# A decoder layer on one core: the last two column chunks of the last down projection by seven products

## The chip, the core and the metric

One of the eight cores of a Trainium2 chip runs the whole kernel. The metric is the device time of one execution in microseconds (us). Engines: TensorE (PE; its loads of stationary data are PEld) multiplies into eight PSUM banks; VectorE (DVE) and ScalarE (ACT) work element by element; GpSimd (POOL) here issues only transfers that add to what their destination holds; SyncE (SP) issues plain transfers. Each engine runs its own list of instructions in order and waits on semaphores.

## The reference, cut to what matters

The layer is attention and then a ConvFFN, on 256 rows of 2048 columns in float32. What the change touches is the last line:

```
h = rms_norm(x, g_ffn)
u = h @ w_up                        # 2048 x 11264
conv = sum(wc[t] * shift(u, t)) + b_conv
gate, val = split(conv)
x = x + (silu(gate) * val) @ w_down # 5632 x 2048
```

## The kernel before

**Float32 from three products.** Every operand is kept as a high part (rounded to the multiplier's format) and a low part (the difference). A product of a 128x128 block of activations with a 128x512 block of weights is three matmuls: high with high, high with low of the weights, low of the activations with high. ScalarE rounds each weight tile (`high`, w_hi), VectorE makes the difference (`low`, w_lo), both six units ahead of TensorE (`RING = 6`). A weight tile is 256 rows by 512 columns, 512 KB.

**The down projection.** The 5632 hidden columns are 11 blocks of 512 (`BLOCKS`), counted 0 to 10. Of each block, the product with w_down has four column chunks of 512, each of two units ("D", block, u): u = 0..7, chunk u // 2, half u % 2 of the block's 512 hidden columns. A unit is 2 row tiles x 2 blocks of 128 hidden columns x 3 = 12 matmuls, and its weight tile is `w_down[block, u]`. The sums of a chunk are added by VectorE (`add_down`) to `xr`, the residual stream in SBUF (part of `work`), and for the last block SyncE then stores them.

**Seven products.** The up projection already uses a scheme with seven products in place of eight, on 2x2 blocks: activations (rows 0-127 or 128-255, by two column groups) and weights (two sides by two groups). Its steps are called P1 to P7. Some need sums of activations, made by VectorE, then rounded by ScalarE and split by VectorE (`part_high`/`part_low`, `make_more` in block 1); some need sums of weight tiles, made in the buffers `x_at` and `y_at` (raw_x, raw_y, and parts of odd and work), by VectorE or by GpSimd's adding transfers. P1, P6 and P5 add up in one bank, and ScalarE copies out what it holds after P1 and after P6 before the next one writes there. In block 1 half a plain unit stands between P6 and P5.

**What sets the order.** `ffn_units` writes out by hand one list of units for the whole feed-forward part, and every engine walks that list. At unit n, ScalarE and VectorE first do what empties banks, then round and split the weights of unit n + 6, then what else stands at that unit (convolution taps, hidden activations). At the end stand block 9's down units 2 to 7 (from its unit 3 on nothing between them), then block 10's units 0 to 7. Block 10's hidden activations are made meanwhile: VectorE's `hidden` and `hidden_low` and ScalarE's `hidden_high` stand at block 9's units 3 and 4.

**Loads.** `LOADS` are the units with plain tiles; six slots take them in turn (softmax, consts_sb, raw 0 to 3), and SyncE issues a slot's next load when VectorE has split the tile in it.

Of the kernel before, what the change touches and what calls it, by code (L numbers as in the profile page):

```python
# [6 lines left out]
P = 128  # L7
SEQ = 256
RT = SEQ // P
# [192 lines left out]

def ffn_units():
# [46 lines left out]
    units += [("D", BLOCKS - 1, u) for u in range(UPR)]  # L250
# [6 lines left out]
LOADS = [unit for unit in FFN if unit[0] != "S"]  # L257
# [14 lines left out]
def slot_of(k):  # L272
    return FIRST_SLOTS[k % len(FIRST_SLOTS)]

# [43 lines left out]
def decoder_layer(nc, x, x_t, smalls, consts, w_in, w_fox, w_dil, w_out, w_up, w_down, decay_dram, out):  # L318
# [15 lines left out]
    with ctx:  # L334
# [125 lines left out]
        def last_half(name, half):  # L460

            if name in LAST_OWN:
                return own_more[:, LAST_OWN.index(name), :, half * P:half * P + P]
            return actB[:, 12:14, half * SEQ + P:half * SEQ + 2 * P]

# [126 lines left out]
        def _(sp):  # L592
# [64 lines left out]
            def load_unit(unit):  # L657
# [4 lines left out]
                elif unit[0] == "D":  # L662
                    src = w_down[unit[1], unit[2], :, :]
                else:
# [102 lines left out]
            for k in range(RAW_SLOTS):  # L767
                sp.wait_ge(lo_done, FF_UNIT - RAW_SLOTS + k)
                load_unit(LOADS[2 + k])
            for n, unit in enumerate(FFN, FF_UNIT):  # L770
                if unit[0] != "S":
# [13 lines left out]
                elif name == "P2" and i + 1 < BLOCKS:  # L785
# [21 lines left out]
            for c in range(4):  # L807
                for r in range(RT):
                    sp.wait_ge(d_added, 8 * (BLOCKS - 1) + 2 * c + r + 1)
                    sp.dma_start(out_rows[:, r, c * NB:(c + 1) * NB], xr[:, r, c * NB:(c + 1) * NB])\  # L810
                        .then_inc(out_done, 16)
# [4 lines left out]
        def _(pe):  # L816
# [460 lines left out]
            def down_pair(i, c):  # L1277

                at = 4 * (i - BLOCKS + 2) + c
                pairs = {2: (0, 1), 3: (2, 3), 4: (5, 6), 5: (0, 1), 6: (2, 3), 7: (4, 7)}.get(at, (5, 6))  # L1280
                return bank[pairs[0]], bank[pairs[1]]

            def down_unit(n, i, u):
# [3 lines left out]
                if u % 2 == 0:  # L1287
# [5 lines left out]
                    elif i == BLOCKS - 1 and c < 3:  # L1293
                        pe.wait_ge(d_added, 8 * i - 4 + 2 * c)
                    elif i == BLOCKS - 1:
                        pe.wait_ge(conv_done, 2 * BLOCKS)
# [4 lines left out]
                last = i == BLOCKS - 1 and u == UPR - 1  # L1301
# [3 lines left out]

            for n, unit in enumerate(FFN, FF_UNIT):
                if unit[0] == "D":
# [35 lines left out]
        def _(act):  # L1343
            def high(n):
# [24 lines left out]
                elif FFN[n - FF_UNIT][0] != "S":  # L1369
                    k = LOAD_AT[FFN[n - FF_UNIT]]  # L1370
                    src = raw_at[slot_of(k)]
                    act.wait_ge(w_loaded[slot_of(k)], 16 * load_count(k))
                else:
# [489 lines left out]

            for n, unit in enumerate(FFN, FF_UNIT):
                running_sum(n, unit)
                down_out(n, unit)
                if unit == ("U", 1, 1, 0):
                    seed_down(0, 0)
# [13 lines left out]
                elif unit == ("U", 0, 1, 0):  # L1882
                    act.wait_ge(warm, 2)
                    nc.scalar.activation(st[:, 91:92], st[:, 90:91], ACT.Silu)
                if unit[0] == "D":
# [58 lines left out]
        def _(dve):  # L1944
            def low(n):
# [9 lines left out]
                elif FFN[n - FF_UNIT][0] != "S":  # L1955
                    src = raw_at[slot_of(LOAD_AT[FFN[n - FF_UNIT]])]
                else:
# [5 lines left out]
                if (pair and name == "P2"  # L1963
                        or n >= FF_UNIT and FFN[n - FF_UNIT][2] == "P2" and not fourth_by_transfer(i, q)):
                    dve.wait_ge(lo_done, n)
                    nc.vector.tensor_tensor(y_at[q], y_at[q], x_at[q], ALU.add).then_inc(y_added[q], 1)
                elif (n >= FF_UNIT and FFN[n - FF_UNIT][2] == "P7"
                      or pair and name == "P7"):
# [484 lines left out]
            def down_banks(i, c):  # L2453

                at = 4 * (i - BLOCKS + 2) + c
                pairs = {2: (0, 1), 3: (2, 3), 4: (5, 6), 5: (0, 1), 6: (2, 3), 7: (4, 7)}.get(at, (5, 6))
                return bank[pairs[0]], bank[pairs[1]]

            def add_down(n, i, c):

                row0 = i == BLOCKS - 1 and c == 3
# [49 lines left out]

            for n, unit in enumerate(FFN, FF_UNIT):
                empty_banks(n, unit)
# [4 lines left out]
                low(n + RING)  # L2518
                if unit[0] == "D":
# [166 lines left out]


# [53 lines left out]
```

## Time and profile before

| | us |
|---|---|
| median of three runs (lowest, highest) | 1333.23 (1333.12, 1333.65) |
| the profiled execution's own time | 1333.53 |
| its span, first to last instruction | 1331.6 |
| TensorE busy | 1326.6 (100%), 6043 matmuls recorded |
| VectorE busy | 1139.4 (86%) |
| ScalarE busy | 953.0 (72%) |
| GpSimd busy | 161.0 (12%) |

A busy TensorE means that a matmul is somewhere in its pipeline; the spacing of starts tells how fast it runs. The chain of waits says which work ended last at each moment, followed back from the end. In a timeline a row's first number is the start from the span's beginning, the second how long the instruction took; instructions of one engine overlap a little at their ends, so the distance between starts is what one costs in a row of them. A bracket at a row's end is the engine's idle time before it and what ended it.

### The profile page before, as it was taken

The page shows a single profiled execution, that of the slowest core. Times are in us where ns is not written, and L with a number is a line of the kernel's source. Part 1 is how long each engine was busy: PE and PEld are TensorE (multiplying, and loading weights), DVE is VectorE, ACT ScalarE, POOL GpSimd, SP SyncE. Part 2 cuts the span into 40 slices and gives each one's busy share as a digit, 9 for nine tenths or more (in the row PEclk, how much of TensorE's full clock was granted, in tenths as well). Part 3 has the DMA queues.
Part 4 walks back from the last instruction along what each step waited for, and adds up shares of the span by engine and source line. Part 5 has one row for each costly group of instructions (what it writes and reads, how often), then busy time and mean ns, then how long its engine had stood idle before and what let it go on. Part 6 is the DMA issues. An engine that isn't in the chain of part 4 may idle for free.

```text
span 1331.6 us, 16497 instructions
## 1 busy us (share of the span) xinstructions
PE 1326.6 (100%) x6043; PEld 1100.1 (83%) x6043; DVE 1139.4 (86%) x1355; ACT 953.0 (72%) x1201; POOL 161.0 (12%) x179
## 2 busy tenths in 40 slices
PE   9999999999999999999999999999999999999998
PEld 7888888888888888888888888888888888888887
DVE  6868787888877876888688898999999999999996
ACT  6666666666665654667777878888888888888872
POOL 0121212021011000101010101111111102020200
PEclk9999999999999999999999999999999999999999
DMA  9877685758888665597879798999989899999952
GB/s 358 281 177 259 143 262 118 244 153 229 229 219 225 219 214 197 128 316 204 268 179 324 165 298 177 309 226 278 249 246 270 231 288 216 303 206 311 205 197 95
DMA packets 119007, 306.78 MB, mean 230 GB/s; under 512 B 11912, under 2 KB 13200, under 8 KB 118672
## 3 DMA queue, kind: packets, MB, share of 16 engines
q1 hardware_dynamic: 91760, 233.53, 50.6%
q0 software_dynamic: 22816, 68.17, 29.0%
q10 hardware_dynamic: 4352, 4.05, 1.0%
q8 instruction: 48, 0.79, 0.2%
q14 instruction: 31, 0.25, 0.1%
HBM read 303.60 MB, written 2.11 MB: 230 GB/s over the span
## 4 chain that ended last, share of the span: by engine, by line
PE 98%; DMA 0%; DVE 0%; ACT 0%; issue 0%; POOL 0%; ACTq 0%; POOLq 0%
PE acc L826 12%; PE acc L830 12%; PE acc L828 12%; PE acc L866 9%; PE acc L870 9%; PE acc L868 9%; PE acc L1053 4%; PE acc L1057 4%; PE acc L1055 4%; PE acc L1032 3%; PE acc L1028 3%; PE acc L1030 3%; PE acc L1220 1%; PE acc L851 1%; PE acc L847 1%; PE acc L849 1%
## 5 line engine op out<-in xcount | busy, mean ns | idle before, releaser
L1961 DVE TENSOR_TENSOR w_lo<-raw,w_hi 128x1024 fp32r<-128x1024 f32 x225 | 273.2, 1222 | 66.8 <-ACT w_hi L1396 66.0
L1396 ACT ACTIVATE w_hi<-raw 128x1024 fp32r<-128x1024 f32 x225 | 235.2, 1054 | 87.5 <-PE acc L830 49.4
L826 PE MATMUL acc<-w_hi,actA 128*128 128x512 f32 x596 | 234.7, 394 | 0.0
L830 PE MATMUL acc<-w_hi,actA 128*128 128x512 f32 x596 | 232.4, 390 | 0.0
L828 PE MATMUL acc<-w_lo,actA 128*128 128x512 f32 x596 | 232.0, 389 | 0.0
L1396 ACT ACTIVATE w_hi<-raw_y 128x1024 fp32r<-128x1024 f32 x152 | 158.1, 1058 | 76.4 <-PE acc L830 22.2
L1961 DVE TENSOR_TENSOR w_lo<-raw_y,w_hi 128x1024 fp32r<-128x1024 f32 x152 | 183.0, 1221 | 21.2 <-ACT w_hi L1396 19.6
L1961 DVE TENSOR_TENSOR w_lo<-raw_x,w_hi 128x1024 fp32r<-128x1024 f32 x114 | 137.6, 1223 | 44.7 <-ACT w_hi L1396 44.5
L1396 ACT ACTIVATE w_hi<-raw_x 128x1024 fp32r<-128x1024 f32 x114 | 117.5, 1051 | 42.9 <-DMA raw_x<-w_in 21.2
L830 PEld LDWEIGHTS acc<-w_hi,actA 128*128 128x128 f32 x596 | 111.9, 188 | 23.7
L828 PEld LDWEIGHTS acc<-w_lo,actA 128*128 128x128 f32 x596 | 112.0, 188 | 22.5
L826 PEld LDWEIGHTS acc<-w_hi,actA 128*128 128x128 f32 x596 | 111.9, 188 | 22.5 <-issue 0.2
L866 PE MATMUL acc<-w_hi,actB 128*128 128x512 f32 x296 | 116.1, 392 | 0.0
L870 PE MATMUL acc<-w_hi,actB 128*128 128x512 f32 x296 | 115.3, 389 | 0.0
L868 PE MATMUL acc<-w_lo,actB 128*128 128x512 f32 x296 | 115.2, 389 | 0.0
L1053 PE MATMUL acc<-w_hi,actA 128*128 128x512 f32 x224 | 88.3, 394 | 0.0
L1057 PE MATMUL acc<-w_hi,actA 128*128 128x512 f32 x224 | 87.3, 390 | 0.0
L1055 PE MATMUL acc<-w_lo,actA 128*128 128x512 f32 x224 | 87.2, 389 | 0.0
L1396 ACT ACTIVATE w_hi<-odd 128x1024 fp32r<-128x1024 f32 x63 | 66.3, 1053 | 19.0 <-PE acc L870 9.8
L1961 DVE TENSOR_TENSOR w_lo<-odd,w_hi 128x1024 fp32r<-128x1024 f32 x63 | 76.9, 1221 | 1.8 <-ACT w_hi L1396 1.8
L2437 DVE SCALAR_TENSOR_TENSOR work<-acc,smalls_sb,work 128x255 f32<-128x255 f32 (+1 forms) x176 | 72.6, 478 | 3.4 <-ACT work L1779 3.3
L2668 POOL DMA_DIRECT2D raw_y<-w_up x34 | 29.5, 867 | 377.0 <-DVE w_lo L1961 376.8
(344 smaller groups left out, 2739.2 us busy)
## 6 DMA issues: line engine op xcount, KB each, us to landing
raw<-w_in SPq DMA_DIRECT2D x101, 512.0 KB, 4.8
raw<-w_down SPq DMA_DIRECT2D x59, 512.0 KB, 5.7
raw_x<-w_up SPq DMA_DIRECT2D x44, 512.0 KB, 4.9
raw_y<-w_up POOLq DMA_DIRECT2D x34, 512.0 KB, 7.3
raw_x<-w_in SPq DMA_DIRECT2D x28, 512.0 KB, 3.9
odd<-w_up SPq DMA_DIRECT2D x27, 512.0 KB, 5.2
work<-w_up SPq DMA_DIRECT2D x24, 512.0 KB, 5.5
work<-w_up POOLq DMA_DIRECT2D x24, 512.0 KB, 8.0
```

Source lines behind the costliest of these rows:

```text
L826: nc.tensor.matmul(o, lhsT=a_h, rhs=w_hi[:, s, k, :], start=first and k == 0, stop=False, skip_group_check=onto_seed)
L828: nc.tensor.matmul(o, lhsT=a_h, rhs=w_lo[:, s, k, :], start=False, stop=False, skip_group_check=onto_seed)
L830: mm = nc.tensor.matmul(o, lhsT=a_l, rhs=w_hi[:, s, k, :], start=False, stop=last and k == KU - 1, skip_group_check=onto_seed)
L866: nc.tensor.matmul(o, lhsT=a_h, rhs=w_hi[:, s, k, :], start=first and k == 0, stop=False, skip_group_check=True)
L868: nc.tensor.matmul(o, lhsT=a_h, rhs=w_lo[:, s, k, :], start=False, stop=False, skip_group_check=True)
L870: mm = nc.tensor.matmul(o, lhsT=a_l, rhs=w_hi[:, s, k, :], start=False, stop=last and k == KU - 1, skip_group_check=True)
L1053: nc.tensor.matmul(o, lhsT=a_h, rhs=w_hi[:, s, k, :], start=side == 0 and j == 0 and k == 0, stop=False, skip_group_check=True)
L1055: nc.tensor.matmul(o, lhsT=a_h, rhs=w_lo[:, s, k, :], start=False, stop=False, skip_group_check=True)
L1057: mm = nc.tensor.matmul(o, lhsT=a_l, rhs=w_hi[:, s, k, :], start=False, stop=kt == KT - 1, skip_group_check=True)
L1396: nc.scalar.activation(w_hi[:, n % RING, :, :], src.rearrange("p (k n) -> p k n", k=KU), ACT.Copy).then_inc(hi_done, 1)
L1961: nc.vector.tensor_tensor(w_lo[:, n % RING, :, :], src.rearrange("p (k n) -> p k n", k=KU), w_hi[:, n % RING, :, :].bitcast(f32), ALU.subt ...
L2437: t = nc.vector.scalar_tensor_tensor(out=conv[:, j, lag:SEQ], in0=bank[(4, 7)[j // 2]][:, (j % 2) * SEQ:(j % 2 + 1) * SEQ - lag], scalar=s ...
```

## The change

Block 10's units 4 to 7 (chunks 2 and 3, four plain units) go. In their place stand seven products ("T", 10, name), in the order P1, P7, P6, P5, P2, P4, P3, between units 0, 1 (chunk 0) and units 2, 3 (chunk 1), which are now last. A product is one 128-row block by 256 hidden columns: 6 matmuls.

```
     units += [("D", BLOCKS - 2, u) for u in range(LATE - 1, UPR)]
-    units += [("D", BLOCKS - 1, u) for u in range(UPR)]
+    units += [("D", BLOCKS - 1, u) for u in range(2)]
+    units += [("T", BLOCKS - 1, name) for name in TAIL_STEPS]
+    units += [("D", BLOCKS - 1, u) for u in range(2, LATE)]
+TAIL_STEPS = ("P1", "P7", "P6", "P5", "P2", "P4", "P3")
+TAIL_BANKS = {"P1": 4, "P6": 4, "P5": 4, "P7": 7, "P4": 7, "P2": 2, "P3": 5}
+TAIL_TILE = {"P1": 4, "P2": 5, "P3": 7}
+TAIL_SUMS = {"P4": (0, (7, 6, 4, 5)), "P6": (1, (7, 6, 4)), "P7": (2, (7, 6)), "P5": (3, (4, 6))}
+TAIL_STORES = ((0, 0), (1, 0), (1, 3), (0, 2), (1, 2), (0, 3), (0, 1), (1, 1))
```

P1, P2 and P3 use plain tiles (4, 5, 7) out of the six slots. The other four use sums of two to four tiles, signs being left to the activations and to the adds at the end. A sum's first tile is loaded by SyncE into `x_at[q]` when that buffer's last use is over, the others are added to it by GpSimd, first one for all four sums, then the second and third:

```
+                elif name == "P2":
+                    if fourth_by_transfer(i, q):
+                        sp.wait_ge(lo_done, n)
+                    else:
+                        sp.wait_ge(y_added[q], added_before(i, q) + 2)
+                    load_tail_base(q)
...
+            for more in range(3):
+                for q, tiles in TAIL_SUMS.values():
+                    if more + 1 >= len(tiles):
+                        continue
...
+                    nc.gpsimd.dma_start(x_at[q], w_down[BLOCKS - 1, tiles[more + 1], :, :], accum_op=ALU.add)\
+                        .then_inc(x_summed[q], 16)
```

VectorE makes four sums of activations (`make_tail`), ScalarE rounds five parts (`tail_high`, into own_parts and wf), VectorE splits them (`tail_low`):

```
+                if unit == ("D", BLOCKS - 2, UPR - 2):
+                    make_tail()
+                elif unit == ("D", BLOCKS - 2, UPR - 1):
+                    for part in ("P1", "P7", "P6"):
+                        tail_low(part)
+                elif unit == ("D", BLOCKS - 1, 0):
+                    for part in ("P5", "P3"):
+                        tail_low(part)
```

TensorE waits at the products, and ScalarE copies banks between them:

```
+            def tail_product(n, name):
+                if name == "P1":
+                    pe.wait_ge(conv_done, 2 * BLOCKS)
+                elif name == "P6" or name == "P2":
+                    pe.wait_ge(p1_copied, BLOCKS + 1)
+                elif name == "P5":
+                    pe.wait_ge(g_v, PAIRS + 2)
+                elif name == "P4":
+                    pe.wait_ge(g_v7, PAIRS + 2)
+                elif name == "P3":
+                    pe.wait_ge(d_seeded, seeds_before(BLOCKS - 2, 0) + 1)
+                if name in TAIL_PARTS:
+                    pe.wait_ge(h_part_lo, 8 + TAIL_PARTS.index(name) + 1)
+                pe.wait_ge(lo_done, n)
...
+            def tail_copy(n, name):
+                act.wait_ge(used, n + 1)
+                if name == "P1":
+                    act.wait_ge(d_added, 8 * (BLOCKS - 1))
+                    nc.scalar.activation(bank[2], bank[4], ACT.Copy, scale=-1.0).then_inc(p1_copied, 1)
+                elif name == "P7":
+                    nc.scalar.activation(tmp[:, 1, :], bank[7], ACT.Copy).then_inc(g_v7, 1)
+                elif name == "P5":
+                    act.wait_ge(d_seeded, seeds_before(BLOCKS - 2, 0) + 1)
+                    nc.scalar.activation(xr[:, 0, 3 * NB:], bank[4], ACT.Copy).then_inc(g_u0, 1)
+                else:
+                    nc.scalar.activation(tmp[:, 0, :], bank[4], ACT.Copy, scale=-1.0).then_inc(g_v, 1)
```

Bank 5, which P3 fills, is first loaded by ScalarE with the residual; six one-bank sums on VectorE (`tail_sums`) replace the four two-bank adds of chunks 2 and 3.

VectorE's list before, from the adds of block 9's chunk 2 on (acc is PSUM, work holds the residual; w_lo rows are weight differences, of block 10's units 3 to 7):

```order
L2470 TENSOR_TENSOR work<-acc,work 128x512 [waits unit_used]
L2470 TENSOR_TENSOR work<-acc,work 128x512
L1961 TENSOR_TENSOR w_lo<-raw,w_hi 128x1024 [waits hi_done] x2
L2470 TENSOR_TENSOR work<-acc,work 128x512 [waits unit_used]
L2470 TENSOR_TENSOR work<-acc,work 128x512
L1961 TENSOR_TENSOR w_lo<-raw,w_hi 128x1024 [waits hi_done]
L1961 TENSOR_TENSOR w_lo<-softmax,w_hi 128x1024 [waits hi_done]
L2470 TENSOR_TENSOR work<-acc,work 128x512 [waits unit_used]
L2470 TENSOR_TENSOR work<-acc,work 128x512
L1961 TENSOR_TENSOR w_lo<-consts_sb,w_hi 128x1024 [waits hi_done]
```

and now (L2636 to L2641 are the four sums, L2649 the low part of P1's activations; the w_lo rows are those of P7, P6 and P5):

```order
L2590 TENSOR_TENSOR work<-acc,work 128x512 [waits unit_used]
L2590 TENSOR_TENSOR work<-acc,work 128x512
L2082 TENSOR_TENSOR w_lo<-odd,w_hi 128x1024 [waits hi_done]
L2082 TENSOR_TENSOR w_lo<-raw_x,w_hi 128x1024 [waits hi_done]
L2636 TENSOR_TENSOR work<-work 128x256 [waits a_ready]
L2638 TENSOR_TENSOR work<-work 128x256 [waits h_made]
L2639 TENSOR_TENSOR work<-work 128x256
L2641 TENSOR_TENSOR work<-work 128x256 [waits h_made]
L2590 TENSOR_TENSOR work<-acc,work 128x512 [waits unit_used]
L2590 TENSOR_TENSOR work<-acc,work 128x512
L2082 TENSOR_TENSOR w_lo<-work,w_hi 128x1024 [waits hi_done]
L2649 SCALAR_TENSOR_TENSOR own_parts<-work,own_parts 128x2x128 [waits h_part_hi]
```

The weight differences keep their places; between them and the adds stand the four sums, and the low part for P1 comes behind P5's weights.

ScalarE's list before, from the rounding of block 10's hidden activations (L1803) on; the w_hi rows are the weights of units 3 to 7:

```order
L1803 ACTIVATE actA<-work 128x4x256 [waits unit_used,a_ready]
L1396 ACTIVATE w_hi<-raw 128x1024 [waits unit_used,w_loaded1]
L1396 ACTIVATE w_hi<-raw 128x1024 [waits unit_used,w_loaded2]
L1396 ACTIVATE w_hi<-raw 128x1024 [waits unit_used,w_loaded3]
L1396 ACTIVATE w_hi<-softmax 128x1024 [waits unit_used,w_loaded8]
L1396 ACTIVATE w_hi<-consts_sb 128x1024 [waits unit_used,w_loaded9]
```

and now, from P6's weights (raw_x) on (L1956 are the five parts, L1964, L1966 and L1971 the copies of P1, P7 and P6; w_hi rows: P6, P5, P2, P4, P3, unit 2):

```order
L1482 ACTIVATE w_hi<-raw_x 128x1024 [waits unit_used,x_summed1]
L1956 ACTIVATE own_parts<-work 128x2x128 [waits a_ready]
L1956 ACTIVATE wf<-work 128x2x128 [waits h_made]
L1956 ACTIVATE own_parts<-work 128x2x128 [waits h_made] x3
L1482 ACTIVATE w_hi<-work 128x1024 [waits unit_used,x_summed3]
L1482 ACTIVATE w_hi<-raw 128x1024 [waits unit_used,w_loaded1]
L1482 ACTIVATE w_hi<-raw_x 128x1024 [waits unit_used,x_summed0]
L1964 ACTIVATE acc<-acc 128x512 [waits d_added,unit_used]
L1482 ACTIVATE w_hi<-raw 128x1024 [waits unit_used,w_loaded2]
L1966 ACTIVATE tmp<-acc 128x512 [waits unit_used]
L1482 ACTIVATE w_hi<-raw 128x1024 [waits unit_used,w_loaded3]
L1971 ACTIVATE tmp<-acc 128x512 [waits unit_used]
```

The five parts stand before P5's weights, and each copy has the rounding of a later unit's weights in front of it.

## Rows read from the trace of the kernel before

**Rows 1.** The page, part 4: shares of the chain that ended last.

```profile
PE 98%; DMA 0%; DVE 0%; ACT 0%; issue 0%; POOL 0%; ACTq 0%; POOLq 0%
```

**Rows 2.** Timeline, TensorE, last block: start us, us, engine, line, operation.

```profile
1306.21 0.39 PE L826 MATMUL acc<-w_hi,actA 128*128 128x512 f32 x1
...
1311.65 0.39 PE L826 MATMUL acc<-w_hi,actA 128*128 128x512 f32 x1
...
1327.74 0.39 PE L830 MATMUL acc<-w_hi,actA 128*128 128x512 f32 x1
```

**Rows 3.** Timeline, VectorE, last 30 us of the program.

```profile
1304.38 1.23 DVE L2450 TENSOR_TENSOR actA<-work,actA 128x1024 fp32r<-128x1024 f32 x1
1305.52 1.28 DVE L2470 TENSOR_TENSOR work<-acc,work 128x512 f32<-128x512 f32 x2
1306.72 2.35 DVE L1961 TENSOR_TENSOR w_lo<-raw,w_hi 128x1024 fp32r<-128x1024 f32 x2
1308.98 1.28 DVE L2470 TENSOR_TENSOR work<-acc,work 128x512 f32<-128x512 f32 x2
...
1328.16 0.69 DVE L2470 TENSOR_TENSOR work<-acc,work 128x512 f32<-128x512 f32 x1 [0.67 <-PE acc L830]
```

**Rows 4.** Timeline, ScalarE, the same stretch.

```profile
1303.29 1.06 ACT L1803 ACTIVATE actA<-work 128x1024 fp32r<-128x1024 f32 x1 [3.92 <-DVE work L2446]
```

**Rows 5.** Timeline, VectorE, block 1: the same four sums, for other products.

```profile
706.90 0.43 DVE L2057 TENSOR_TENSOR odd<-work 128x256 f32<-128x256 f32 x1
...
707.70 0.42 DVE L2060 TENSOR_TENSOR odd<-work 128x256 f32<-128x256 f32 x1
708.15 0.42 DVE L2062 TENSOR_TENSOR odd<-work,odd 128x256 f32<-128x256 f32 x1
```

**Rows 6.** Timeline, ScalarE, block 1: the roundings of those sums.

```profile
708.67 0.42 ACT L1480 ACTIVATE actB<-odd 128x256 fp32r<-128x256 f32 x1 [1.33 <-DVE odd L2062]
708.99 0.40 ACT L1480 ACTIVATE actB<-work 128x256 fp32r<-128x256 f32 x1
```

**Rows 7.** Timeline, all engines, block 1: P5 waits for the copy of P6.

```profile
695.32 0.39 PE L870 MATMUL acc<-w_hi,actB 128*128 128x512 f32 x1
...
695.68 1.06 ACT L1396 ACTIVATE w_hi<-raw 128x1024 fp32r<-128x1024 f32 x1
...
696.63 0.69 ACT L1815 ACTIVATE tmp<-acc,st 128x512 f32<-128x512 f32 x1
...
697.37 0.19 PEld L866 LDWEIGHTS acc<-w_hi,actA 128*128 128x128 f32 x1 [0.66 <-ACT tmp L1815]
...
697.71 0.40 PE L868 MATMUL acc<-w_lo,actA 128*128 128x512 f32 x1
```

**Rows 8.** Timeline, ScalarE: a copy from one bank to another.

```profile
1248.93 0.60 ACT L1812 ACTIVATE acc<-acc 128x512 f32<-128x512 f32 x1
1249.45 2.01 ACT L1396 ACTIVATE w_hi<-raw_y 128x1024 fp32r<-128x1024 f32 x2
```

**Rows 9.** Timeline, SyncE's queue, before the last tiles.

```profile
1268.25 2.60 SPq L668 DMA_DIRECT2D raw<-w_down  x2
1285.78 0.33 SPq L668 DMA_DIRECT2D softmax<-w_down  x1
```

**Rows 10.** Timeline, VectorE: last uses of the pair buffers.

```profile
1270.40 2.37 DVE L1961 TENSOR_TENSOR w_lo<-raw_x,w_hi 128x1024 fp32r<-128x1024 f32 x2
...
1276.34 1.22 DVE L1961 TENSOR_TENSOR w_lo<-work,w_hi 128x1024 fp32r<-128x1024 f32 x1
```

**Rows 11.** The page, part 6: adding transfers; KB each, us to landing.

```profile
work<-w_up POOLq DMA_DIRECT2D x24, 512.0 KB, 8.0
```

**Rows 12.** Timeline, TensorE, start of the program.

```profile
1.31 4.21 PE L953 MATMUL acc<-actB 128*128 128x512 f32 x9 [1.31 <-POOL actB L2613]
5.32 0.63 PE L924 MATMUL acc<-w_hi,actA 128*128 128x512 f32 x1
...
7.68 0.39 PE L924 MATMUL acc<-w_hi,actA 128*128 128x512 f32 x1
```

More of the change, by code:

```diff
@@ L256 @@
 UNITS = FF_UNIT + len(FFN)
-LOADS = [unit for unit in FFN if unit[0] != "S"]
+LOADS = [unit for unit in FFN if unit[0] in ("U", "D", "O") or unit[0] == "T" and unit[2] in TAIL_TILE]
 LOAD_AT = {unit: m for m, unit in enumerate(LOADS)}
@@ L273, in slot_of, with tail_sum_loads, tail_sum_adds @@
     return FIRST_SLOTS[k % len(FIRST_SLOTS)]
+def tail_sum_loads(q):
+    return 2 * uses_before(BLOCKS, q) + 1
+def tail_sum_adds(q):
+    return uses_before(BLOCKS, q) + next(len(tiles) - 1 for at, tiles in TAIL_SUMS.values() if at == q)
 def next_in_slot(k):
@@ L663, in load_unit @@
                     src = w_down[unit[1], unit[2], :, :]
+                elif unit[0] == "T":
+                    src = w_down[unit[1], TAIL_TILE[unit[2]], :, :]
                 else:
@@ L769, in _, with load_tail_base @@
                 load_unit(LOADS[2 + k])
+            def load_tail_base(q):
+                base = next(tiles[0] for at, tiles in TAIL_SUMS.values() if at == q)
+                sp.dma_start(x_at[q], w_down[BLOCKS - 1, base, :, :]).then_inc(x_loaded[q], 16)
             for n, unit in enumerate(FFN, FF_UNIT):
+                if unit[0] == "T" and unit[2] not in TAIL_TILE:
+                    continue
                 if unit[0] != "S":
@@ L1304, in down_unit @@
                           row0_done if last else None, seeded(i))
+            def tail_product(n, name):
[12 more added lines that the diff above has]
+                pe.wait_ge(lo_done, n)
+                o = bank[TAIL_BANKS[name]]
+                s = n % RING
+                for k in range(KU):
+                    if name in TAIL_PARTS:
+                        part = tail_part(name)[:, k, :]
+                        a_h, a_l = part[:, 0:P], part[:, P:2 * P]
+                    else:
+                        kt, at = KU + k, P if name == "P4" else 0
+                        a_h = hidden_of(BLOCKS - 1)[:, kt, at:at + P]
+                        a_l = hidden_of(BLOCKS - 1)[:, kt, SEQ + at:SEQ + at + P]
+                    first = name in ("P1", "P7") and k == 0
+                    nc.tensor.matmul(o, lhsT=a_h, rhs=w_hi[:, s, k, :], start=first, stop=False,
+                                     skip_group_check=True)
+                    nc.tensor.matmul(o, lhsT=a_h, rhs=w_lo[:, s, k, :], start=False, stop=False,
+                                     skip_group_check=True)
+                    mm = nc.tensor.matmul(o, lhsT=a_l, rhs=w_hi[:, s, k, :], start=False, stop=k == KU - 1,
+                                          skip_group_check=True)
+                mm.then_inc(used, 1)
             for n, unit in enumerate(FFN, FF_UNIT):
+                if unit[0] == "T":
+                    tail_product(n, unit[2])
+                    continue
                 if unit[0] == "D":
@@ L2512, in _ @@
             for n, unit in enumerate(FFN, FF_UNIT):
-                empty_banks(n, unit)
+                last_adds = unit[0] == "D" and unit[1] == BLOCKS - 1
+                if not last_adds:
+                    empty_banks(n, unit)
                 if unit == ("S", 0, "P5", QU - 1):
```

121 lines of the change are left out of this document (103 added, 18 removed).

## The prediction

> **What bounds the kernel now.** I read the page's chain of waits first: TensorE holds 98% of what ended last [rows 1], so time is matmuls times their spacing, plus whatever makes TensorE stand still. Then the timeline of TensorE alone over the tail. The reader is to see that it never pauses there: the first matmul of the last block's down projection starts at 1306.21, the first of its unit 2 (where the change begins) at 1311.65, and the very last at 1327.74 [rows 2], 95 matmuls later, so one each (1327.74 - 1306.21) / 95 = 0.2266 us. A unit of 12 is 2.72 us, one of the new products (6 matmuls) 1.36 us. Third, the timelines of VectorE and ScalarE over the same stretch, for what they finish just in time. VectorE goes from one instruction into the next from 1304.38 on with no idle time in its rows [rows 3]; its difference for the hidden activations ends at 1304.38 + 1.23 = 1305.61, and TensorE takes it at 1306.21. That is 0.60 us of slack on an engine that has no pause behind it; whatever the change puts behind it starts late. Last, SyncE's queue and the page's DMA issues, for the new transfers.
>
> **What goes.** Two chunks by four plain units are 48 matmuls; seven products are 42. Six matmuls less: 6 x 0.2266 = 1.36 us. That is all TensorE can win; the last add, the store and what follows them keep their place: from the last matmul at 1327.74 to the add at 1328.16 [rows 2, 3] and the end of the span at 1331.6.
>
> **What is added in front of the first product (P1).** P1 may start only when the low half of its activations is made. Up to the plain unit 1 the order on TensorE is the old one, so it is wanted at 1311.65 [rows 2]. In VectorE's new order that low half stands behind: the adds of chunk 2, two weight differences (P7, P6), four sums, the adds of chunk 3, and the weight difference of P5; and that last one waits for ScalarE, which must first round five sums (and then P5's weights), of which four wait for VectorE's sums. Step by step:
> - The order is unchanged through the adds of chunk 2 at 1305.52; the next two weight differences take 1306.72 to 1308.98, as the two that stand there today do [rows 3]. ScalarE rounds their weights right behind the hidden activations (1303.29 + 1.06) [rows 4], in time.
> - The four sums begin at 1308.98. The same four at 706.90: the third starts 0.80 us after the first and lasts 0.42 [rows 5], so ScalarE's second rounding (for P7, the one that needs the third sum) is released at 1310.20. From the fourth sum's end there (708.15 + 0.42) to ScalarE's start at 708.67 [rows 5, 6] is 0.10: 1310.30.
> - Four roundings at 0.32 each (708.99 - 708.67) [rows 6]: 1311.58. P5's weights, 1.06 [rows 7]: 1312.64. VectorE has long finished the adds of chunk 3 and waits here.
> - ScalarE to VectorE 0.03 (1303.29 + 1.06 to 1304.38) [rows 3, 4]; the weight difference until the next instruction starts, 1.14 (1304.38 to 1305.52) [rows 3]; the low half 0.42 as the sums: 1314.23.
> - TensorE's restart. In block 1 the copy ends at 696.63 + 0.69 = 697.32 and the second matmul after it starts at 697.71, which puts the first, at full spacing, at 697.48: 0.16 us [rows 7]. P1 starts at 1314.39.
> Stall: 1314.39 - 1311.65 = 2.74 us. Each link has its row, but for another tile; I bound it by 2.3 (a link or two overlapping better) and 3.1 us.
>
> **What is added between P6 and P5.** Both accumulate in bank 4, and ScalarE must copy out P6's value before P5 writes there. In the order of TensorE nothing stands between them. Count from P1's start t. P1's last matmul starts at t + 1.13; a reader starts 0.42 after such a start (1327.74 to 1328.16) [rows 2, 3]: the first copy at t + 1.55. Copies hold ScalarE 0.52 us (1248.93 to 1249.45) [rows 8], weight roundings 0.95 (695.68 to 696.63) [rows 7]. Its program goes copy, rounding, copy, rounding, copy: 1.55, 2.07, 3.02, 3.54, 4.49, and the last copy ends 0.60 later [rows 8], t + 5.09. P6 itself was ready to be read at t + 4.27; the rounding in front costs 0.22. With the restart of 0.16 P5 begins at t + 5.25, wanted at t + 18 x 0.2266 = t + 4.08: stall 1.17 us. From below: the copy straight after P6 would still be 0.42 + 0.60 + 0.16 less the spacing, 0.95. From above: block 1, where P5 starts (697.48) 1.93 us after P6's last matmul would have given way (695.32 + 0.23), a whole rounding standing in front [rows 7]; half a plain unit fills most of that wait there, nothing does here.
>
> **What is hidden.** P6 needs the copy of P1, done at t + 2.15, restart 2.31; wanted at t + 2.72. Weights of the later products and their sums run 2 us or more ahead of TensorE once it has lost 2.7. The six one-bank adds on VectorE end before the last plain unit does. The stores keep their queue.
>
> **Transfers.** Four base loads stand on SyncE between 1268.25 and 1285.78, where it issues nothing today [rows 9]; the first can go when VectorE has split the last use of its buffer, 1270.40 + 1.2 [rows 10]. Seven adding transfers follow on GpSimd's queue, which has no work left. At 8.0 us each [rows 11], and 8.0 for the base too, the longest sum (P4: four tiles) lands at 1271.6 + 4 x 8.0 = 1303.6, with issue time about 1307; ScalarE asks for it near 1313.4. The other bases go by 1276.34 + 1.22 = 1277.6 at the latest [rows 10]; P7's sum (two tiles) and P6's (three) are asked for near 1304.3 and 1305.3 and are there by 1293.6 and 1301.6. I cost the transfers at nothing. What they could disturb is the loads of SyncE's next two tiles (1285.78 on): a rival below.
>
> **Sum.** 2.74 + 1.17 - 1.36 = +2.55 us on the profiled execution's 1333.53: 1336.1. That execution lies 0.30 above the median of the three runs, 1333.23, so the forecast is 1335.8. By the bounds: 2.3 + 0.95 - 1.36 = +1.9 to 3.1 + 1.93 - 1.36 = +3.7, that is 1335.1 to 1336.9. A measurement of this kernel tells about 0.2%, 2.67 us, from no change, which is 1335.9: the forecast sits just under that line and its own range lies on both sides.
>
> **Rivals.**
> - *The gain comes through.* If P1's low half were ready by 1311.49 and the copy of P6 were covered, the time would be 1333.23 - 1.36 = 1331.9. For it: VectorE and ScalarE each have idle time later in the tail. Against: both waits follow from the fixed order of the instructions, with durations in rows. One of the two waits short by a microsecond or more gives 1333.0 to 1335.0. Chance 9% together, nearly always within 0.2%.
> - *VectorE comes late to the hidden activations already.* The new transfers share the DMA engines with the next two loads; the tile issued at 1285.78 [rows 9] is split by VectorE long before TensorE wants it, but in VectorE's order it stands before the hidden activations. Should a load hold VectorE up by 1 to 2 us, everything from 1304.38 on moves by it, one for one (the 0.60 us of slack does not help P1, whose chain runs through VectorE): 1336.8 to 1337.8. Against: the adding transfers come one at a time per buffer and mostly end before. Chance 9%.
> - *The clock falls.* At the start of the program TensorE, idle before 1.31, runs nine matmuls in (5.32 - 1.31), 0.45 us each, and one takes 0.63; at 7.68 one takes 0.39 as in the tail [rows 2, 12]. The slow ones fit 512 columns at 1.2 GHz (0.43), the tail's spacing fits 2.4 GHz; the granted clock reads 1.00 all the same, so the spacing tells. The tail of before has no stop; the one in block 1 is 0.50 us with no slow matmul behind it [rows 7]. If 2.7 us of standing still brought the low level back for as long as at the start, some 6 us, about 14 matmuls would cost 0.20 each: +2.8 on the forecast, 1338.6. It decides only if that one stop is enough. Chance 8%.
> The Trainium skill ("TensorE: Matmul & The Clock Gate", Part 1) says that the slow rate is the default, that an idle spell brings it back and that sustained work releases it. By that rule the last rival's time is 1338.6, without it 1335.8; the trace agrees as to the start, and no run here shows a stop of 2.7 us.
>
> **Chances.** The forecast's mechanism, both stalls: 74%, of which a little under half above 1335.9. Slower: 0.33 + 0.09 + 0.08 = 0.50. Same: 0.41 + 0.07 = 0.48. Faster by 0.2% would need 2.67 us, twice what goes: 0.02. Range for 8 in 10: 1334.4 (one stall partly covered) to 1337.5 (a late VectorE on top).
>
> **What would show it.** Right: TensorE idle about 2.7 us before the first matmul of P1, released by VectorE's low half, and VectorE idle before P5's weight difference, waiting for ScalarE; TensorE idle about 1.17 us before P5, released by ScalarE's copy to tmp; all else at 0.2266. Wrong in the first step: the first plain unit of the last block later than 1306.3 (VectorE or a load), or P1 with no wait. Wrong in the second: P5 straight behind P6. Clock: matmuls 0.43 us apart behind a stall. Transfers: ScalarE idle with raw_x, odd or work from w_down as the releaser.

## The result and the profile after

| | before | after |
|---|---|---|
| median (lowest to highest), us | 1333.25 (1333.12 to 1334.5), 6 runs | 1339.92 (1336.78 to 1340.91), 6 runs |
| the profiled execution's time, us | 1333.53 | 1336.78 |
| its span, us | 1331.6 | 1335.0 |
| TensorE busy, matmuls recorded | 1326.6 us, 6043 | 1326.1 us, 6037 |
| bytes moved, MB | 306.78 | 312.03 |

The change makes the kernel slower: ratio 1.0043, interval 1.0032 to 1.0053; 6.7 us between the medians, 5.8 between the means. The forecast was 1335.8 (1334.4 to 1337.5), so the sign was right and the time lies outside the range. One number needs a word: the profiled execution of after is the lowest of the six. Its mean granted clock (the share of TensorE's full 2.4 GHz that it was given) is 1.000; in the others it is 0.997 to 0.999. So the trace below explains 1336.78, and the 3.1 us up to the median need other traces and runs (e1, e2, e4, e7).

TensorE's timeline of after, where [rows 2] had no pause at all: start, duration, instruction, idle time before it and what ended it.

```profile
1306.92 0.50 PE L873 MATMUL acc<-w_hi,actA 128*128 128x512 f32 x1 [0.71 <-DVE actA L2570]
...
1312.28 0.39 PE L877 MATMUL acc<-w_hi,actA 128*128 128x512 f32 x1
1315.48 0.47 PE L1377 MATMUL acc<-w_hi,own_parts 128*128 128x512 f32 x1 [2.82 <-issue]
...
1319.42 0.39 PE L1381 MATMUL acc<-w_hi,own_parts 128*128 128x512 f32 x1
1320.64 0.50 PE L1377 MATMUL acc<-w_hi,own_parts 128*128 128x512 f32 x1 [0.83 <-ACT tmp L1971]
...
1331.43 0.39 PE L877 MATMUL acc<-w_hi,actA 128*128 128x512 f32 x1
```

Three stops where there were none: before block 10's first unit, before P1 (L1377 after 1312.28), before P5 (1320.64). Between them starts are 0.23 us apart, as before, but for the first behind each stop (0.31 to 0.35).

VectorE, answering [rows 3] and [rows 5]:

```profile
1298.02 1.23 DVE L2082 TENSOR_TENSOR w_lo<-consts_sb,w_hi 128x1024 fp32r<-128x1024 f32 x1 [0.63 <-ACT w_hi L1482]
1299.85 3.34 DVE L2557 SCALAR_TENSOR_TENSOR work<-acc,smalls_sb,work 128x255 f32<-128x255 f32 x8 [0.60 <-ACT work L1865]
...
1305.65 1.23 DVE L2570 TENSOR_TENSOR actA<-work,actA 128x1024 fp32r<-128x1024 f32 x1
...
1310.25 0.42 DVE L2636 TENSOR_TENSOR work<-work 128x256 f32<-128x256 f32 x1
...
1313.82 1.22 DVE L2082 TENSOR_TENSOR w_lo<-work,w_hi 128x1024 fp32r<-128x1024 f32 x1 [0.69 <-ACT w_hi L1482]
1314.96 0.42 DVE L2649 SCALAR_TENSOR_TENSOR own_parts<-work,own_parts 128x256 fp32r<-128x256 f32 x1
```

ScalarE, answering [rows 4] and [rows 6]:

```profile
1296.93 1.06 ACT L1482 ACTIVATE w_hi<-consts_sb 128x1024 fp32r<-128x1024 f32 x1 [2.72 <-DMA consts_sb<-w_down]
...
1311.50 0.42 ACT L1956 ACTIVATE wf<-work 128x256 fp32r<-128x256 f32 x1 [3.69 <-DVE work L2639]
...
1312.74 1.04 ACT L1482 ACTIVATE w_hi<-work 128x1024 fp32r<-128x1024 f32 x1
```

The middle of the chain is the one the prediction wrote down: the sums at 1310.25 release the roundings at 1311.50, those hold up the rounding of P5's weights (1312.74), VectorE waits for it (0.69) and only then makes P1's low half (1314.96, L2649). It ends at 1314.96 + 0.42 = 1315.38, and P1 starts 0.10 us later; the profile itself names no releaser there ("issue"). But VectorE is late before that begins: the hidden activations' difference starts at 1305.65, and at 1304.38 before [rows 3]. The two waits above it, 0.63 and 0.60, make that up, and both lead to ScalarE at 1296.93, which waited 2.72 us for a load. The DMA view, 1276 to 1300 us, of before and then of after (queues: packets, MB, share of 16 engines; issues: KB each, median us to landing):

```profile
q1 hardware_dynamic: 982, 3.60, 45.4%
...
softmax<-w_down SPq DMA_DIRECT2D x2, 512.0 KB, 3.9
consts_sb<-w_down SPq DMA_DIRECT2D x2, 512.0 KB, 4.5
```

```profile
q0 software_dynamic: 759, 2.78, 61.9%
q1 hardware_dynamic: 894, 3.26, 37.7%
...
softmax<-w_down SPq DMA_DIRECT2D x2, 512.0 KB, 10.8
consts_sb<-w_down SPq DMA_DIRECT2D x1, 512.0 KB, 10.1
```

Before, the DMA engines were idle more than half of the time here; with the adding transfers (q0) they are full. The medians above mix loads of several units. Taken singly, the loads of block 10's first two units (softmax, issued at 1285.63, and consts_sb, at 1286.77) land in 7.5 and 10.1 us; before they took 3.3 and 4.2.

**The profiled execution against the sum.** P1 starts at 1315.48; the prediction's chain gave 1314.39: +1.09, which is VectorE's 1.27 at 1305.65 less 0.18 by which the chain from the four sums on was shorter than forecast. From P1 to P5 5.16 us, predicted 5.25: -0.09. From P5 to the last matmul 10.79 against 47 x 0.2266 = 10.65: +0.14. From the last matmul to the end of the execution 1336.78 - 1331.43 = 5.35 against 5.79 before: -0.44. Together +0.70 on the 1336.08 of the sum: 1336.78. The last term was not forecast. In all seven traces with the seven adding transfers this end takes 5.34 or 5.35 us, in the five without them (before, e2, e4, e9, e11) 5.69 to 5.82; why is not shown.

### The profile page after: what moved, and what is told of

Same layout as the page of the kernel before. It is cut to its first block, busy times and chain, and to the rows that moved or that the text cites. A ratio compares the mean times of both kernels' runs of the same rounds, so it can differ in the third digit from the quotient of the medians.

```text
span 1335.0 us, 16536 instructions
## 1 busy us (share of the span) xinstructions
PE 1326.1 (99%) x6037; PEld 1099.4 (82%) x6037; DVE 1148.0 (86%) x1369; ACT 960.2 (72%) x1214; POOL 167.0 (13%) x186
## 2 busy tenths in 40 slices
DMA packets 120448, 312.03 MB, mean 234 GB/s; under 512 B 12072, under 2 KB 13360, under 8 KB 120112
## 4 chain that ended last, share of the span: by engine, by line
PE 92%; DVE 5%; DMA 1%; ACT 1%; issue 1%; POOL 0%; ACTq 0%; DVEq 0%; POOLq 0%
PE acc L873 11%; PE acc L877 11%; PE acc L875 11%; PE acc L913 8%; PE acc L917 8%; PE acc L915 8%; PE acc L1104 4%; PE acc L1100 4%; PE acc L1102 4%; PE acc L1077 3%; PE acc L1079 3%; PE acc L1075 3%; DVE w_lo L2082 3%; PE acc L898 1%; PE acc L894 1%; PE acc L896 1%
## 5 line engine op out<-in xcount | busy, mean ns | idle before, releaser
L873 PE MATMUL acc<-w_hi,actA 128*128 128x512 f32 x580 | 228.8, 395 | 0.7 <-DVE actA L2570 0.7
L877 PE MATMUL acc<-w_hi,actA 128*128 128x512 f32 x580 | 226.4, 390 | 0.0
L875 PE MATMUL acc<-w_lo,actA 128*128 128x512 f32 x580 | 226.0, 390 | 0.0
L873 PEld LDWEIGHTS acc<-w_hi,actA 128*128 128x128 f32 x580 | 109.0, 188 | 22.9 <-DVE actA L2570 1.1
L877 PEld LDWEIGHTS acc<-w_hi,actA 128*128 128x128 f32 x580 | 108.9, 188 | 23.0
L875 PEld LDWEIGHTS acc<-w_lo,actA 128*128 128x128 f32 x580 | 109.1, 188 | 21.8
L1100 PE MATMUL acc<-w_hi,actA 128*128 128x512 f32 x224 | 88.5, 395 | 0.0
L1104 PE MATMUL acc<-w_hi,actA 128*128 128x512 f32 x224 | 87.4, 390 | 0.0
L1102 PE MATMUL acc<-w_lo,actA 128*128 128x512 f32 x224 | 87.3, 390 | 0.0
```

The costliest lines, as they stand in the source:

```text
L873: nc.tensor.matmul(o, lhsT=a_h, rhs=w_hi[:, s, k, :], start=first and k == 0, stop=False, skip_group_check=onto_seed)
L875: nc.tensor.matmul(o, lhsT=a_h, rhs=w_lo[:, s, k, :], start=False, stop=False, skip_group_check=onto_seed)
L877: mm = nc.tensor.matmul(o, lhsT=a_l, rhs=w_hi[:, s, k, :], start=False, stop=last and k == KU - 1, skip_group_check=onto_seed)
L1100: nc.tensor.matmul(o, lhsT=a_h, rhs=w_hi[:, s, k, :], start=side == 0 and j == 0 and k == 0, stop=False, skip_group_check=True)
L1102: nc.tensor.matmul(o, lhsT=a_h, rhs=w_lo[:, s, k, :], start=False, stop=False, skip_group_check=True)
L1104: mm = nc.tensor.matmul(o, lhsT=a_l, rhs=w_hi[:, s, k, :], start=False, stop=kt == KT - 1, skip_group_check=True)
```

## The experiments

Two theories were open: T1, the adding transfers delay loads and by that VectorE; T2, the clock falls behind a stop, so that TensorE runs for a while at 1.2 GHz in place of 2.4. Each run's own runs of the kernel before, on the same chip, are its measure: medians 1333.95 for e1 to e4, 1333.53 for e6 to e9, 1333.69 for e10 and e11. A ratio is to those runs, with its 95% interval; differences are between medians.

**e1_again: the changed kernel, unedited, for another trace.**

> The changed kernel once more, to see where a typical execution loses its time (the profiled one, 1336.8 us, was the fastest of six). Theory T1 (transfers): the seven adding transfers keep the DMA engines full from 1280 to 1308, the loads of block 10's first two tiles land late by a varying amount, and TensorE stops longer before unit 0 of block 10 (0.7 us in the fastest execution, 3 to 5 us in a slow one), clock 1.000 in what follows. Theory T2 (clock): the stops are as in the fastest execution, but behind the one at P1 the matmuls come 0.43 us apart for a while and the mean granted clock is below 1.000. Either way 1337 to 1341 us.

1339.24 us (1338.6 to 1340.05), ratio 1.0038 (1.0024 to 1.0053), +5.3. Its profiled execution, 1338.66, has the same three stops, and then this, TensorE behind the stop before P1:

```profile
1315.81 0.47 PE L1377 MATMUL acc<-w_hi,own_parts 128*128 128x512 f32 x1 [2.78 <-issue]
1316.11 0.42 PE L1379 MATMUL acc<-w_lo,own_parts 128*128 128x512 f32 x1
1316.35 0.61 PE L1381 MATMUL acc<-w_hi,own_parts 128*128 128x512 f32 x1
1316.76 0.63 PE L1377 MATMUL acc<-w_hi,own_parts 128*128 128x512 f32 x1
...
1319.32 0.60 PE L1377 MATMUL acc<-w_hi,wf 128*128 128x512 f32 x1
1319.75 0.41 PE L1379 MATMUL acc<-w_lo,wf 128*128 128x512 f32 x1
```

and the same stretch as busy time (start and end, length, PE, PEld, DVE, ACT, POOL, then the granted clock, DMA share, GB/s):

```profile
1315.00:1320.00 5.00, 4.19 (x12) 3.31 (x13) 5.00 (x10) 2.55 (x4) 0.00 (x0) 0.66 0.00 0
```

From 1316.35 to 1319.75 eight starts take 3.40 us where 8 x 0.2266 = 1.81 would do: 1.59 us lost, at 0.425 each, which is 512 columns at 1.2 GHz, and the granted clock of the 5 us reads 0.66 (0.50 over these 3.40 us alone). T2 is shown for this execution, and is most of the 1.88 us between it and after's profiled one. It is not all that varies: another of the five took 1338.6 at a mean clock of 1.000.

**e2_no_adds: no adding transfers.** Each weight sum stays at its first tile, so the last two chunks of the output are other numbers; instructions on the engines are the same.

```
-                    act.wait_ge(x_summed[q], 16 * tail_sum_adds(q))
+                    act.wait_ge(x_loaded[q], 16 * tail_sum_loads(q))
-            for more in range(3):
+            for more in range(0):
```

> The changed kernel without its seven adding transfers: the four sums are their first tile alone, so the last two column chunks come out different. T1: the loads land as in the kernel before, no stop before unit 0, 1333.25 + 2.55 = 1335.8 us, executions within 0.5 us of each other. T2: the stops at P1 (2.7 us) and P5 (1.2 us) are still there, so the clock falls as before: 1337 to 1340 us with a mean clock of 0.997 to 0.999.

1337.49 us (1335.76 to 1338.67), ratio 1.0025 (1.0016 to 1.0034), +3.5, so 1.8 less than e1. Its profiled execution, 1335.76 at clock 1.000, is the case the forecast described. VectorE, then TensorE:

```profile
1304.26 1.23 DVE L2570 TENSOR_TENSOR actA<-work,actA 128x1024 fp32r<-128x1024 f32 x1
```

```profile
1311.33 0.39 PE L877 MATMUL acc<-w_hi,actA 128*128 128x512 f32 x1
1314.10 0.47 PE L1377 MATMUL acc<-w_hi,own_parts 128*128 128x512 f32 x1 [2.38 <-issue]
...
1318.08 0.39 PE L1381 MATMUL acc<-w_hi,own_parts 128*128 128x512 f32 x1
1319.28 0.50 PE L1377 MATMUL acc<-w_hi,own_parts 128*128 128x512 f32 x1 [0.81 <-ACT tmp L1971]
```

VectorE is on time (1304.26), nothing stops before the first unit, and the two stops cost 1314.10 - 1311.33 - 0.23 = 2.54 and 1319.28 - 1318.08 - 0.23 = 0.97 us (2.63 and 1.09 up to the second matmul, which follows 0.31 and 0.34 behind the first). T1 is shown. The median is the one of T2: the four executions at clock 1.000 have a median of 1336.6, 2.7 over before, where the forecast had 2.55; the six below 1.000 one of 1337.75.

**e3_parts_early: the activations' sums and low halves earlier in VectorE's order**, ahead of the adds of chunk 3 and of P5's weight difference.

```
                 if unit == ("D", BLOCKS - 2, UPR - 2):
-                    make_tail()
-                elif unit == ("D", BLOCKS - 2, UPR - 1):
                     for part in ("P1", "P7", "P6"):
                         tail_low(part)
...
                         hidden_low(BLOCKS - 1)
+                        make_tail()
```

> The changed kernel with the parts of the activations made earlier on VectorE: the four sums straight behind the hidden activations, the low parts of P1, P7 and P6 before the adds of chunk 3. The stop at P1 goes (or falls below 0.5 us), the one at P5 stays. By the rows of the fastest execution: 1336.8 - 2.7 = about 1334.1 us. T1: executions still spread by some 4 us, up to 1338, since the transfers are the same. T2: 1334 to 1335, mean clock 1.000, spread under 1 us, since no stop is as long as 2.7 us.

1334.16 us (1333.18 to 1335.78), ratio 1.0001 (0.9991 to 1.001), +0.2; the clock is 1.000 in all ten executions. TensorE:

```profile
1307.13 0.50 PE L873 MATMUL acc<-w_hi,actA 128*128 128x512 f32 x1 [0.94 <-DVE actA L2570]
...
1312.47 0.40 PE L877 MATMUL acc<-w_hi,actA 128*128 128x512 f32 x1
1312.71 0.39 PE L1377 MATMUL acc<-w_hi,own_parts 128*128 128x512 f32 x1
...
1316.57 0.39 PE L1381 MATMUL acc<-w_hi,own_parts 128*128 128x512 f32 x1
1317.94 0.50 PE L1377 MATMUL acc<-w_hi,own_parts 128*128 128x512 f32 x1 [0.99 <-ACT tmp L1971]
```

P1 follows at full spacing; the other two stops stand. Taking away one stop, 2.97 us in after's timeline, gained 5.1 against e1, and with it went the falls of the clock. Time and clock are those of T2; the spread, 2.6 us, lies between the two forecasts.

**e4_stop: the kernel before with one stop added.** TensorE waits before chunk 1 of block 10 for three ScalarE copies into buffers no longer in use; nothing of the computation changes.

```
+                        if c == 1:
+                            pe.wait_ge(stop, 1)
...
+                if unit == ("D", BLOCKS - 1, 1):
+                    act.wait_ge(used, n + 1)
+                    act.wait_ge(a_ready, BLOCKS)
+                    nc.scalar.activation(work[:, 0:768], work[:, 1024:1792], ACT.Copy)
+                    nc.scalar.activation(work[:, 768:1024], work[:, 1024:1280], ACT.Copy)
+                    nc.scalar.activation(softmax[:, UNIT:UNIT + P], work[:, 1024:1152], ACT.Copy).then_inc(stop, 1)
```

> The kernel before with one stop of TensorE and nothing else: the first matmul of block 10's unit 2 waits for three ScalarE instructions that do nothing for the result, about 2.7 us. T1: 1333.25 + 2.7 = 1336.0 us, clock 1.000, executions within 0.5 us. T2: more than that, 1337.5 to 1341, a mean clock of 0.997 to 0.999 and a spread of some us between executions.

1337.7 us (1336.07 to 1338.86), ratio 1.0023 (1.0014 to 1.0033), +3.75. TensorE in its profiled execution (1336.47, clock 1.000):

```profile
1311.58 0.39 PE L831 MATMUL acc<-w_hi,actA 128*128 128x512 f32 x1
1314.42 0.50 PE L827 MATMUL acc<-w_hi,actA 128*128 128x512 f32 x1 [2.45 <-ACT softmax L1888]
```

Here the stop costs 1314.42 - 1311.58 - 0.23 = 2.61, with the late second matmul (0.33) 2.7, and nothing more. The ten executions part by their mean clock: three at 1.000 take 1336.07 to 1336.80 (median 1336.47), seven at 0.998 or 0.999 take 1336.13 to 1338.86 (median 1337.99). Of the 80 runs of the kernel before beside e1 to e11, two are below 1.000. No trace was taken of an e4 execution with slow matmuls; by clocks and times, a bare stop of this length, with none of the change, is enough for the clock to fall, in most executions and not in all.

**e6_p2_first: e3, and P2 moved between P6 and P5.** P2 fills bank 2, so the copy of bank 4 runs beside it; two stores change places.

```
-TAIL_STEPS = ("P1", "P7", "P6", "P5", "P2", "P4", "P3")
+TAIL_STEPS = ("P1", "P7", "P6", "P2", "P5", "P4", "P3")
```

> On top of e3_parts_early, the product P2 (which needs no bank that ScalarE has just read) stands between P6 and P5. Theory (the stop before P5 is ScalarE's copy of P6's bank, and lies on the path): the 1.0 us that e3 showed before P5 goes, the 0.9 us before the first unit of block 10's last projection stays, and the time is e3's 1334.2 less 1.0, 1333.2 us (1332.8 to 1333.6). Rival (the tail only just keeps pace, so that the wait moves on to another product, P4 or P3): 1334.2 us, with a stop of about 1 us further down.

1332.8 us (1331.42 to 1333.38), ratio 0.9992 (0.9983 to 1.0001), -0.7, that is 0.94 less than e3 against its own before. In the trace no product stops any more, and this is the only wait left:

```profile
1306.11 0.50 PE L873 MATMUL acc<-w_hi,actA 128*128 128x512 f32 x1 [0.17 <-DVE actA L2570]
```

The 0.9 us expected to stay here are 0.17; e3's trace has 0.94 with the same transfers, so the lateness differs from execution to execution. The stop before P5 was worth about what it measured, as far as intervals of over 1 us to each side tell, and did not move on. The interval of e6 reaches 1.0001: it cannot be told from the kernel before.

**e7_hold: e6, and the adding transfers in another order.**

```
+            for name in ("P7", "P6", "P5", "P6", "hold", "P4", "P4", "P4"):
+                if name == "hold":
+                    k = LOAD_AT[("D", BLOCKS - 1, 1)]
+                    pool.wait_ge(w_loaded[slot_of(k)], 16 * load_count(k))
+                    continue
```

> On top of e6, the adding transfers go in another order: P7's, P6's first, P5's, P6's second, and P4's three only once the weights of block 10's second unit have landed. Theory (the adding transfers keep the loads of the last units' weights back, and VectorE is late by that): those loads land in about 4 to 6 us instead of 10, the 0.9 us before the first unit shrinks to 0.3 or less, and the time is 1331.9 (the 6 matmuls less alone) to 1332.6 us, faster than the kernel before. Rival (VectorE is late by the tail's own parts and not by loads): the stop stays at 0.9 and the time at e6's 1333.2. Second rival (held back, P4's sums come too late): a stop of over 1 us before P4, 1334 us or more.

1336.08 us (1333.48 to 1337.93), ratio 1.0018 (1.0009 to 1.0027): the second rival. ScalarE, then TensorE:

```profile
1315.37 1.06 ACT L1482 ACTIVATE w_hi<-raw_x 128x1024 fp32r<-128x1024 f32 x1 [4.90 <-DMA raw_x<-w_down]
1316.33 0.58 ACT L1964 ACTIVATE acc<-acc 128x512 f32<-128x512 f32 x1
```

```profile
1314.28 0.39 PE L1381 MATMUL acc<-w_hi,wf 128*128 128x512 f32 x1
1316.96 0.50 PE L1377 MATMUL acc<-w_hi,own_parts 128*128 128x512 f32 x1 [2.29 <-ACT acc L1964]
...
1318.99 0.63 PE L1377 MATMUL acc<-w_hi,actA 128*128 128x512 f32 x1
1319.41 0.63 PE L1379 MATMUL acc<-w_lo,actA 128*128 128x512 f32 x1
```

The first unit no longer stops, but P4's sum (raw_x) lands 4.90 us after ScalarE asks for it. Behind that rounding stands the copy of P1's bank, which P6 needs, so P6 is late by 2.3 us, and the clock falls again (0.42 between starts, granted clock 0.50 from 1318 to 1321). I had looked for the damage at P4; it came at P6, through ScalarE's order.

**e8_hold_only: the changed kernel with e7's order of transfers alone** (the edit above).

> The changed kernel with this order of the adding transfers alone; parts and products stay as in the change. Theory (transfers delay the loads): as without adding transfers, 1337.5 us (1336.5 to 1338), no stop before the first unit, 2.4 to 2.8 before P1, and the clock still falls behind that in most executions. Rival (any adding transfer in this stretch costs, whatever its order): 1339.2 us.

1336.84 us (1334.84 to 1339.06), ratio 1.0024 (1.0015 to 1.0033), +3.3: as e2 (+3.5), with every byte moved. There is no stop before the first unit, 2.38 before P1, and 0.83 before P5:

```profile
1314.30 0.47 PE L1377 MATMUL acc<-w_hi,own_parts 128*128 128x512 f32 x1 [2.38 <-issue]
```

What counted was when the transfers run, not that they run. P4's late sum (ScalarE waits 1.29 us for it) does no harm here, where TensorE is late itself.

**e9_short_stop: e4 with one copy in the place of three.**

```
-                    nc.scalar.activation(work[:, 0:768], work[:, 1024:1792], ACT.Copy)
-                    nc.scalar.activation(work[:, 768:1024], work[:, 1024:1280], ACT.Copy)
```

> The kernel before with one stop of TensorE in e4's place that is about half as long (one short ScalarE operation in the place of three), 1.2 to 1.5 us. Theory (the clock falls behind a long stop, not behind one of about 1 us): it costs its own length alone, 1335.1 to 1335.5 us, and the granted clock of every execution is 1.000. Rival (any stop of over 1 us there can take the clock): 1336 us or more, with executions at 0.998.

1335.31 us (1334.47 to 1336.83), ratio 1.0011 (1.0002 to 1.002), +1.78. TensorE stops 1.41 us, and starts are 0.23 apart behind it:

```profile
1312.12 0.39 PE L831 MATMUL acc<-w_hi,actA 128*128 128x512 f32 x1
1313.91 0.50 PE L827 MATMUL acc<-w_hi,actA 128*128 128x512 f32 x1 [1.41 <-ACT softmax L1886]
```

1313.91 - 1312.12 - 0.23 = 1.56, nearly the whole 1.78. Ten of eleven mean clocks are 1.000; the eleventh, 0.999, is this trace. Its tail has no slow matmul: the granted clock reads 1.00 in the tail up to the last matmul (1330.15) and 0.81 from there to the end of the span, where it costs nothing. So a single 0.999 proves no slow matmul; at most 3.9 us lie behind the last matmul in any trace here, at half clock 0.0014 of the whole, so 0.998 and 0.997 are more than that end can make up. This stop costs its length, e4's costs a microsecond more than its length.

**e10_hold_two: e7 with P4's first adding transfer ahead of the hold.**

```
-            for name in ("P7", "P6", "P5", "P6", "hold", "P4", "P4", "P4"):
+            for name in ("P4", "P7", "P6", "P6", "hold", "P4", "P5", "P4"):
```

> e7_hold with P4's first adding transfer among those that go ahead, and two of P4's and P5's held. Theory (e7 lost because P4's third sum came 5 us after ScalarE wanted it, and a 2.3 us stop took the clock with it; the loads themselves no longer made VectorE late): no stop of over 0.3 us is left, and the time is 1331.9 to 1332.6 us, under e6_p2_first by 0.2 to 0.8. Rival (P4's last sum still lands after ScalarE wants it, since two adding transfers in a row take 14 us from 1296): a stop before P5 of 0.5 to 2 us, 1333 to 1335.5 us.

1331.96 us (1331.43 to 1333.09), ratio 0.9989 (0.998 to 0.9998), -1.7: the one version here that computes the whole result and whose interval lies under the kernel before (e11, below, leaves out part). VectorE's hidden activations and TensorE at the places of the three stops:

```profile
1304.71 1.22 DVE L2570 TENSOR_TENSOR actA<-work,actA 128x1024 fp32r<-128x1024 f32 x1
```

```profile
1306.08 0.39 PE L877 MATMUL acc<-w_hi,actA 128*128 128x512 f32 x1
1306.31 0.39 PE L873 MATMUL acc<-w_hi,actA 128*128 128x512 f32 x1
...
1311.52 0.39 PE L877 MATMUL acc<-w_hi,actA 128*128 128x512 f32 x1
1311.75 0.39 PE L1377 MATMUL acc<-w_hi,own_parts 128*128 128x512 f32 x1
...
1317.02 0.39 PE L1381 MATMUL acc<-w_hi,actA 128*128 128x512 f32 x1
1317.24 0.45 PE L1377 MATMUL acc<-w_hi,own_parts 128*128 128x512 f32 x1
...
1326.61 0.39 PE L877 MATMUL acc<-w_hi,actA 128*128 128x512 f32 x1
```

No stop is left, and the last matmul starts at 1326.61, 1.13 us earlier than in [rows 2]: most of the six matmuls' 1.36 us is won here. The profiled execution, 1331.95, is 1.58 under that of before, 1333.53; the other 0.45 is the shorter end.

**e11_no_adds: e6 without the adding transfers** (e2's edit, leaving out the same part of the sums).

> e6_p2_first without the adding transfers: the sums of weights stay at their first tile, so two products' worth of the result differ. Theory (in e6 the transfers still make VectorE late in most executions, 0.2 to 0.9 us before the first unit of the last projection): 1331.9 to 1332.3 us, which is the kernel before less its 6 matmuls, and a spread under 0.6 us. Rival (what e6 still lacks is not the transfers): e6's 1332.8 us.

1332.24 us (1331.48 to 1333.75), ratio 0.9991 (0.9982 to 0.9999), -1.45. That is on the theory's side of e6's -0.7, but the spread is 2.3 us where under 0.6 was expected, and the two intervals overlap: what the transfers still cost in e6 is not settled. In the traces the last matmul starts 0.21 us before e6's, but the end without transfers is 0.34 longer (5.69 against 5.35), which cancels it.

## Why the prediction was wrong

- **The matmuls, 6 x 0.2266 = 1.36: right, as far as the runs tell.** TensorE recorded six fewer, e10's last matmul is 1.13 earlier, and e10 is 1.7 under before, with 1.36 well inside its interval (0.3 to 2.7 us). That what follows the last matmul keeps its place was wrong by 0.44 in after.
- **The stop before P1, 2.74: right in place, cause and size.** 2.54 in e2 (2.63 up to the second matmul, from which the prediction took its restart), 2.97 in after, where VectorE's lateness is in it; moving the parts (e3) removed it.
- **The stop between P6 and P5, 1.17: right in cause, a little large.** 0.97 to 0.99 in e2 and after (1.09 in e2 up to the second matmul); one product between them (e6) removed it.
- **"I cost the transfers at nothing": the first step that failed.** I took the landing of adding transfers from the middle of the kernel [rows 11], found them in time for their own readers, and left what they do to other loads to a rival with 9%. The argument against it, that they come one at a time per buffer, missed that four buffers run at once (by issue and landing, from 1289.2 to 1292.1 in after), that the seven took 8.6 to 14.4 us each and not 8.0, and that an adding transfer holds the DMA engines nearly twice as long per byte. Its mechanism (a load, then ScalarE, then VectorE, then the hidden activations) was the right one, though the load that told was the second (consts_sb); after's execution at clock 1.000, 1336.78, lies at the lower end of its price, 1336.8 to 1337.8. Over the medians the late loads are worth 1.8 to 2 us (e1 against e2 and e8).
- **The clock, 8%: the second.** I called a fall behind one stop unlikely because the half microsecond in block 1 left no slow matmul [rows 7]; that row spoke for short stops only, and a row for 2 to 3 us did not exist. By the Trainium skill ("TensorE: Matmul & The Clock Gate", Part 1) an idle spell brings the slow rate back. The traces of e1 and e7 agree, with 0.43 and 0.42 us between starts behind a stop; four others with stops of 2.38 us and more show none. The rival's size was too large for one fall seen in a trace (1.59 us, not 2.8). To the median it adds 1.0 us in e4, over the stop's own 2.7, and 1.0 in e2, over the forecast's 2.55.
- **The two together.** I held them as separate cases of under a tenth each, so the range ended at 1337.5. Both happened. The runs part them: e2 has the falls of the clock (four of ten executions at 0.998) without the late loads, e3 the late loads without the falls. Forecast, loads and clock are 2.55 + 1.75 + 1.0 = 5.3 us, where e1 measured 5.3. The loads' part is e1 less e2, with e8 (2.0) beside it; the clock's is e2 less the forecast, with e4 beside it.

Not settled: the whole size of the clock's part in after. Its first measurement gave 6.7 us (5.8 between the means) with nearly the same median for after as e1, 1339.92 and 1339.24, and a lower one for before, 1333.25 and 1333.95. In e1 the trace shows 1.59 us; a mean clock of 0.997, which two of after's executions have, is 0.003 x 1335 = 4.0 us, of which part can lie behind the last matmul (e9); one at 0.999 took 1340.4, 3.6 over the lowest, where 0.999 makes up some 1.3, and one of e1's at 1.000 took 1338.6. So something else differs by some 2 us, an estimate from these times. It can be the lateness of the loads, or the scatter that the kernel before has too (1332.96 to 1335.73 beside e1); no trace here is of such an execution.

## What to carry to other kernels

Price a stop of 2 to 3 us, on a TensorE that has had none, for its length and for slow matmuls behind it, even if one trace shows full spacing after it: here two traces of six had the slow matmuls, and removing the stop gave back 5.1 us where the timeline showed 2.97. A mean clock that is a thousandth low may come from behind the last matmul; look where in the trace it is low. Transfers that are in time for their own readers can still delay other loads: look at how full the DMA engines are in that stretch and at the slack of every load issued there. Where an engine's list is fixed, put what the next product waits for ahead of what waits for another engine, and put another bank's product where a copy must empty a bank.

## What the runs showed of the hardware

- Behind stops of 2.78 (e1) and 2.29 us (e7) eight matmuls ran at about half rate, and none behind stops of 2.38 to 2.82 in four other traces (after, e2, e4, e8): the length alone does not decide. Behind stops of 0.7 to 1.4 us (after, e3, e9) the traces have no slow matmul.
- Executions with a mean clock below 1.000: 35 of 53 in the six kernels whose traces have a stop of 2.29 us or more (after, e1, e2, e4, e7, e8), one of 11 in e9 (1.41 us), none of 43 in e3, e6, e10 and e11, and two of 80 in the kernel before.
- In the stretch of after shown above, the adding transfers took 61.9% of 16 engines for 2.78 MB and the plain ones 37.7% for 3.26 MB: 22.3 against 11.6% per MB, 1.9 times as much.
